# Half of the value pages of a paged attention are multiplied in the gated heads instead of in the attention steps

## The reference

```python
mod = silu(c) @ w_ada + b_ada                       # six shifts, scales and gates
h = rms_norm(x) * (1 + scale1) + shift1
q_a, k_a, v_a, q_g, k_g, v_g, og_g, gk_lr, gate_a, gate_b = split(h @ w_in)
o_a = attend(rms_norm(q_a), rms_norm(k_a), v_a)     # 8 heads of 64
o_g, s_new = gla_chunked(q_g, k_g, v_g, log_a, s0)  # 4 heads, 128 keys, 256 values
o_g = rms_norm(o_g) * silu(og_g)
merged = sigmoid(gate_a) * (o_a @ w_branch_a) + sigmoid(gate_b) * (o_g @ w_branch_b)
x = x + gate1 * (merged @ w_out)
x = x + gate2 * hier_moe(rms_norm(x) * (1 + scale2) + shift2)   # 32 experts, two per token
```

## Time and profile before

| | us |
|---|---|
| median of 3 runs | 1307.64 |
| lowest, highest | 1307.28, 1308.71 |
| profiled execution: span from first to last instruction | 1308.1 |
| TensorE busy in the span | 1183.1 |
| DVE, ScalarE, GpSimd busy | 496.8, 234.5, 234.4 |
| HBM traffic | 354.61 MB read, 22.36 MB written |

### The profile page before, as it was taken

One profiled execution on the slowest core, in us unless ns is written; L12 is line 12 of the kernel. 1 busy time (PEld: TensorE's weight loads), 2 busy tenths in 40 slices (PEclk: granted clock), 3 DMA queues, 4 the chain that ended last, 5 costly groups with the idle time before them and its releaser, 6 DMA issues.

```text
span 1308.1 us, 20837 instructions
## 1 busy us (share of the span) xinstructions
PE 1183.1 (90%) x8041; PEld 746.0 (57%) x8041; DVE 496.8 (38%) x1075; ACT 234.5 (18%) x536; POOL 234.4 (18%) x295
## 2 busy tenths in 40 slices
PE   3999998999999999999999997999987788888797
PEld 2344443475767777688888455666644444444464
DVE  3388966522324243454554456322212111111112
ACT  4122235322323232211001222000000000000000
POOL 2432344201102023340000101111111111111001
PEclk9999999999999999999999997999999999999989
DMA  9998999982654635312624627999999999999994
GB/s 352 372 266 287 364 374 385 377 328 65 251 173 144 171 97 131 97 23 57 177 80 178 257 65 209 403 415 419 411 419 416 418 418 418 417 415 418 415 414 161
DMA packets 118393, 368.17 MB, mean 281 GB/s; under 512 B 12604, under 2 KB 58573, under 8 KB 98966
## 3 DMA queue, kind: packets, MB, share of 16 engines
q1 hardware_dynamic: 93408, 304.44, 60.0%
q0 software_dynamic: 21328, 55.24, 13.7%
q10 hardware_dynamic: 3558, 7.13, 1.8%
HBM read 354.61 MB, written 22.36 MB: 288 GB/s over the span
## 4 chain that ended last, share of the span: by engine, by line
PE 67%; DMA 19%; SPq 6%; DVE 3%; issue 2%; ACT 1%; ACTq 0%; DVEq 0%; POOLq 0%
PE ps L1928 64%; DMA ring<-in_w_exp_gate 9%; SPq L549 4%; DMA hx<-in_w_exp_up 3%; PE ps L1939 3%; DMA hx<-in_w_exp_gate 3%; SPq L554 2%; DMA ring<-in_cache_v 1%; DMA hx<-in_shape_table 1%; DMA h_rows<-ring 1%; DVE work L1548 1%; DVE work L1883 0%; DMA work<-h_rows,idx 0%; DVE work L1658 0%; DVE ring L1655 0%
## 5 line engine op out<-in xcount | busy, mean ns | idle before, releaser
L1928 PE MATMUL ps<-ring,work 128*64 128x256 f32 (+4 forms) x2064 | 296.7, 439 | 42.2 <-DMA ring<-in_w_exp_up 16.5
L1928 PE MATMUL ps<-ring,hx 128*32 128x256 f32 (+3 forms) x1552 | 271.1, 443 | 6.7 <-ACT hx L848 4.2
L1928 PEld LDWEIGHTS ps<-ring,work 128*64 128x64 f32 (+2 forms) x2064 | 157.1, 139 | 163.9 <-issue 84.7
L1928 PEld LDWEIGHTS ps<-ring,hx 128*32 128x32 f32 (+1 forms) x1552 | 157.7, 146 | 102.5 <-issue 78.6
L1928 PE MATMUL ps<-hx,ring 128*128 128x272 f32 x704 | 163.8, 393 | 0.6 <-DVE work L1548 0.6
L1928 PE MATMUL ps<-work 128*32 128x256 f32 (+12 forms) x1186 | 134.9, 399 | 21.6 <-DVE work L1240 9.8
L1928 PEld LDWEIGHTS ps<-hx,ring 128*128 128x128 f32 x704 | 133.0, 190 | 28.7 <-DVE work L1548 1.1
L1928 PE MATMUL ps<-hx,work 128*64 128x256 f32 (+2 forms) x784 | 114.2, 413 | 19.8 <-DMA hx<-in_w_exp_up 10.6
L769 POOL DMA_INDIRECT out<-work x32 | 50.5, 1578 | 327.6 <-DVE work L1893 327.6
L1881 DVE TENSOR_TENSOR work<-work,ps 128x256 f32<-128x256 f32 x32 | 13.5, 421 | 250.2 <-ACT work L1185 250.2
L1928 PEld LDWEIGHTS ps<-hx,work 128*64 128x64 f32 (+2 forms) x784 | 67.9, 144 | 66.1 <-issue 26.4
(11 more groups left out here) (337 smaller groups left out, 948.5 us busy)
## 6 DMA issues: line engine op xcount, KB each, us to landing
ring<-in_w_exp_gate SPq DMA_DIRECT2D x21, 2048.0 KB, 40.8
ring<-in_w_exp_down SPq DMA_DIRECT2D x42, 1024.0 KB, 39.0
ring<-in_w_exp_up SPq DMA_DIRECT2D x21, 2048.0 KB, 40.7
ring<-in_w_ada SPq DMA_DIRECT2D x12, 2048.0 KB, 22.4
hx<-in_w_exp_gate SPq DMA_DIRECT2D x11, 2048.0 KB
hx<-in_w_exp_up SPq DMA_DIRECT2D x10, 2048.0 KB, 40.5
work<-in_w_exp_down SPq DMA_DIRECT2D x20, 1024.0 KB
ring<-in_cache_v SPq DMA_DIRECT2D x64, 256.0 KB, 9.3
```

What stands on the lines that cost most here:

```text
L1928: return pe.matmul(out, lhsT, rhs, start=start, stop=stop, **k)
```

## The change

Value blocks 0 to 7 (the first four sequences) are multiplied in attention steps 1, 2, 4, 5, 7, 8, 10 and 11 (`VALUES_AT`). Blocks 8 to 15 move to the gated stage: four in head 2 and four in head 3, at the place where heads 0 and 1 have `late_ada`, into PSUM bank 5. Since a bank can't be held open through the chunks of a head, their sum is kept in SBUF (`late_values`): ScalarE copies the own tokens' part there in step 17, DVE adds the bank in head 2 and again in head 3, keeps each row's head, and TensorE's `selected` stands in head 3. The weights of the later group are transposed in steps 5, 6, 7 (own tokens) and 17 (pages 8 to 15, into banks 4 and 5); `selected` of the first group moves from step 10 to 13. The stream of loads follows: the late blocks come behind the first weights of heads 2 and 3, `SLOT_ORDER` has other buffers there, and all eight pages of a late block are issued by SyncE. On GpSimd two of the four mixtures of `hT` (`hT_mix`) stand further back in head 3, because their place in SBUF holds `late_values` until then.

```diff
-        SLOT_ORDER = ([3, 1, 2, 0, 4, 5, 3] + [1, 2, 0, EXTRA, 4, 1, 2, 0, 4, 1, 5, 2, 0, 4, 1, 5] + [2, 0, 3, 4, 1] * 3 + [2]
-                      + [0, 3, 4, 1, 2, 5] * 2 + [0, 3, 4, 1] + [2, 5, 3, 4, 0, 2, 3, 5] + [4])
+        SLOT_ORDER = ([3, 1, 2, 0, 4, 5, 3] + [1, 2, 0, EXTRA, 4, 1, 2, 0, 4, 1, 5, 2, 0, 4, 1, 5] + [2, 0, 3, 4, 1, 2, 0, 3]
+                      + [4, 1, 2, 0, 3, 5] * 2 + [4, 2, 0, 3, 5, 1] * 2 + [2, 5, 3, 4, 0, 2, 3, 5] + [4])
...
-        for i in range(DEC_B * PAGES // 8):
-            PAGED[("v", i)] = add_block(("v", i), PAGES // 4, (s("pv_s"), i + 1))
+        EARLY_VALUES = PAGES // 2
+
+        def value_block(i):
+            PAGED[("v", i)] = add_block(("v", i), PAGES // 4 if i < EARLY_VALUES else PAGES // 2, (s("pv_s"), i + 1))
+
+        for i in range(EARLY_VALUES):
+            value_block(i)
         GLA = []
...
+            if h >= 2:
+                for i in range(4):
+                    value_block(4 * h + i)
...
+        SHARED_PAGES = [n for (what, i), n in PAGED.items() if what == "k" or i < EARLY_VALUES]
-            if isinstance(stream[n][1], tuple):
-                paged = [m for m in PAGED.values() if SLOT_ORDER[m] == SLOT_ORDER[n] and m <= n]
+            if n in SHARED_PAGES:
+                paged = [m for m in SHARED_PAGES if SLOT_ORDER[m] == SLOT_ORDER[n] and m <= n]
...
-        cT_kept, prT_high, sc_p = xflat[:, 0:KD * 32], xflat[:, 256:1280], xflat[:, 1280:4352].rearrange("p (z o c) -> p z o c", z=3, o=2)
-        late_mod_rows = [xflat[:, 256:768], xflat[:, 768:1280]]
+        cT_kept, prT_low, sc_p = xflat[:, 0:KD * 32], xflat[:, 256:1280], xflat[:, 1280:4352].rearrange("p (z o c) -> p z o c", z=3, o=2)
+        late_mod_rows = [xflat[:, 1280:1792], xflat[:, 1792:2304]]
+        late_values, prT_high = xflat[:, 2816:3328], xflat[:, 3328:4352]
...
-        TURN_AT, SELECT_AT = 5, 10
+        VALUES_AT = {1: 0, 2: 1, 4: 2, 5: 3, 7: 4, 8: 5, 10: 6, 11: 7}
+        LATER_AT, LAST_LATER_AT, SELECT_AT = {5: 0, 6: 1, 7: 4}, 17, 13
...
-                    sp.wait_ge(s("pv_s"), 2 * PAGES // 2)
+                    sp.wait_ge(s("pv_s"), EARLY_VALUES)
-                    load_pages(sp, n, pieces, range(0, 8, 2), slot_sem)
+                    load_pages(sp, n, pieces, range(0, 8, 2) if n in SHARED_PAGES else range(8), slot_sem)
...
+                    pool.wait_ge(s("pv_s"), EARLY_VALUES + 4)
...
+                    if h == GH - 1 and n == 0:
+                        pool.wait_ge(s("o_sel"), 2)
+                        pool.tensor_tensor(hT_mix[:, 2], hT[:, low, first], hT[:, low, last], ALU.subtract).then_inc(s("hT_mixed"), 1)
+                    if h == GH - 1 and n == 1:
+                        pool.wait_ge(s("hT_mixed"), 2)
+                        pool.tensor_tensor(hT_mix[:, 3], hT[:, high, first], hT_mix[:, 1], ALU.subtract).then_inc(s("hT_mixed"), 1)
...
+                if z in LATER_AT:
+                    later_weights(LATER_AT[z])
+                if z == LAST_LATER_AT:
+                    later_weights(2)
+                    later_weights(3)
+                    act.wait_ge(*after("own_late_ps"))
+                    act.activation(late_values, ps[:, 0, :], ACT.Copy).then_inc(*done("own_late"))
...
-            sample_heads(1)
...
+                if h == GH - 1:
+                    sample_heads(1)
...
+                elif h == 2:
+                    dve.wait_ge(*after("own_late"))
+                    dve.wait_ge(s("pv_s"), EARLY_VALUES + 4)
+                    dve.tensor_tensor(late_values, late_values, ps[:, VALUE_BANK, :], ALU.add).then_inc(*done("values_low"))
+                else:
+                    dve.wait_ge(*after("values_low"))
+                    dve.wait_ge(s("pv_s"), EARLY_VALUES + 8)
+                    link(dve.tensor_tensor(late_values, late_values, ps[:, VALUE_BANK, :], ALU.add))
+                    heads_kept(late_values, late_values)
...
+            def own_values(stop):
+                for j in range(4):
+                    last = mm(ps[32 * j:32 * j + 32, 0, :], pr_own[0:NS, 32 * j:32 * j + 32], v_tok[0:NS, PT, :], True, stop,
+                              skip_group_check=True)
+                return last
+
...
+            def late_page_values(first):
+                pe.wait_ge(s("pr_T"), 10)
+                for v in range(first, first + 4):
+                    page_values(v, VALUE_BANK, v == first, v == first + 3)
...
+                if z in LATER_AT:
+                    pe.wait_ge(s("l_norm"), 2)
+                    pe.wait_ge(s("p_ov"), z - 3)
+                    later_weights_turned(LATER_AT[z], 1)
+                if z == LAST_LATER_AT:
+                    pe.wait_ge(s("sc_max"), UNITS - 1)
+                    later_weights_turned(2, 4)
+                    later_weights_turned(3, 5)
...
+                if z == LAST_LATER_AT - 1:
+                    pe.wait_ge(s("o_rows"), 1)
+                    pe.wait_ge(s("pr_T"), 8)
+                    own_values(True).then_inc(*done("own_late_ps"))
+                if z in VALUES_AT:
+                    v = VALUES_AT[z]
+                    if v == 0:
+                        pe.wait_ge(s("pr_T"), 5)
+                        own_values(False)
+                    page_values(v, 0, False, v == EARLY_VALUES - 1)
...
+            pe.wait_ge(s("pr_T"), 10)
...
-            selected(1)
-            pe.wait_ge(s("oa_taken"), 2)
+            pe.wait_ge(*after("own_late"))
...
+                    late_page_values(EARLY_VALUES)
+                else:
+                    late_page_values(EARLY_VALUES + 4)
...
+                        if h == GH - 1:
+                            pe.wait_ge(s("o_rows"), 2)
+                            selected(LATE_BANK, late_values)
...
+                    if i == 0:
+                        pe.wait_ge(*(after("mod_middle") if h == 0 else (s("mod_set"), 2) if h == 1 else after("late_rows") if h == 2 else (s("oa_taken"), 2)))
+                    if i == 0 and h == 2:
+                        pe.wait_ge(*after("values_low"))```

The order of TensorE's instructions, from the scores of step 14 (`ps<-work 128x384`) to the transposes of step 17. `32x512` from `ring` are value blocks, `cst,hx` transposes of the weights, `ring,work 64x128` products with the values. Before:

```order
106 L1928 MATMUL ps<-work 128x384 x2
107 L1928 MATMUL ps<-ring,hx 32x512 x8
108 L1939 MATMUL ps<-cst,hx 128x128 x2
109 L1928 MATMUL ps<-ring,work 64x128 x8
110 L1928 MATMUL ps<-work 128x512 x2
111 L1928 MATMUL ps<-ring,hx 32x512 x8
112 L1939 MATMUL ps<-cst,hx 128x128 x4
113 L1928 MATMUL ps<-ring,work 64x128 x2
114 L1928 MATMUL ps<-ring,hx 32x512 x8
115 L1939 MATMUL ps<-cst,hx 128x128 x6
116 L1928 MATMUL ps<-ring,work 64x128 x4
117 L1939 MATMUL ps<-cst,hx 128x128 x8
```

More of the change, by code:

```diff
@@ L307, in layer_kernel @@
         rbw, far_hot = rbw[0:BUCKETS + 1, 0:P], rbw[0:BUCKETS + 1, P:2 * P]
-        qT, kT, v_tok, near, logit0, logit1, prT_low, pr_own = carve(
+        qT, kT, v_tok, near, logit0, logit1, _, pr_own = carve(
             2176, PAIRS * NT, PAIRS * NT, 5 * AW, AH * 2 * P, PAST + NS, PAST + NS, 2 * 512, P)
@@ L685, in _ @@
                     pool.dma_start(near[COPIES * a:COPIES * a + COPIES], src).then_inc(s("near_in"), 16)
-            for i in range(KEY_BLOCKS):
+            for i in range(EARLY_VALUES):
                 half_pages("v", i)
+            first, last = token_half
+            low, high = GATE_A.low, GATE_A.high
             for h in range(GH):
@@ L696, in _ @@
                     pool.wait_ge(s("late_out"), 64)
-                    first, last = token_half
-                    low, high = GATE_A.low, GATE_A.high
+                    pool.wait_ge(s("pv_s"), EARLY_VALUES + 4)
                     pool.tensor_tensor(hT_mix[:, 0], hT[:, low, last], hT[:, high, last], ALU.add).then_inc(s("hT_mixed"), 1)
@@ L2164, in page_values, with selected @@
                         q = 4 * (page % 2) + j
-                        last = mm(ps[32 * j:32 * j + 32, 0, :], page_weights(g, page)[:, 32 * j:32 * j + 32], slot(n)[:, AW * q:AW * q + AW],
-                                  False, page == PAGES - 1, skip_group_check=True)
+                        last = mm(ps[32 * j:32 * j + 32, bank, :], page_weights(g, page)[:, 32 * j:32 * j + 32], slot(n)[:, AW * q:AW * q + AW],
+                                  start and page == 2 * i, stop and page == 2 * i + 1, skip_group_check=True)
                 last.then_inc(s("pv_s"), 1)
-            def selected(g):
-                pe.wait_ge(s("o_rows"), g + 1)
-                if g:
-                    pe.wait_ge(s("oa_taken"), g)
-                    pe.wait_ge(s("p_T"), UNITS)
-                else:
-                    pe.wait_ge(s("p_ov"), SELECT_AT - 3)
+            def late_page_values(first):
+                pe.wait_ge(s("pr_T"), 10)
+                for v in range(first, first + 4):
+                    page_values(v, VALUE_BANK, v == first, v == first + 3)
+            def selected(bank, rows):
```

(2 more changed lines are left out.)

71 lines of the change are left out of this document (29 added, 42 removed).

## The result

| | before | after |
|---|---|---|
| median of 5 runs each | 1308.71 | 1316.60 |
| lowest, highest | 1307.28, 1313.19 | 1316.00, 1319.60 |
| profiled execution, span | 1308.1 | 1314.8 |
| TensorE, DVE, GpSimd busy in the span | 1183.1, 496.8, 234.4 | 1186.3, 497.6, 217.1 |
| mean granted clock of the profiled execution | 0.982 | 0.978 |

The change makes the kernel slower: ratio 1.0061, 95% interval 1.0046 to 1.0076, which is 6.0 to 9.9 us. The sign is the predicted one, the size is not: 1316.6 lies 5.0 above the forecast of 1311.6 and 1.6 above the top of the range. Of the 5.0, 1.1 is the base: the forecast added its 4 to a median of three runs, 1307.64, and the five runs here have 1308.71. The other 3.9 is the change itself, 7.9 instead of 4.

What follows compares the result with a forecast made beforehand. TensorE was taken as the bound, 67% of the chain of waits. Attention -10.6 and gated heads +15.1 gave +4.5, less 0.5: +4 on a median of 1307.64, so 1311.6 us, range 1307.0 to 1315.0.

Steps and rivals of the forecast that it cites:

- Steps 1 to 11, -6.9: Early attention steps: three blocks' 5.6 us go, 2.2 come back as waits, and some work moves to later steps; net -6.9.
- Steps 12 to 18, -2.6: Last attention steps: blocks -9.3, old waits -1.7, moved groups +3.2, new waits +5.2; net -2.6 us.
- the 0.5 taken off: Taken from the +4.5 sum because the step 12 to 18 walk counts short waits at full length; leaves +4.
- The four waits: New TensorE waits in steps 12 to 18, mostly behind ScalarE's copies: 1.5, 1.3, 1.9 and 0.45, together 5.2 us.
- Behind the steps, -1.1: Between attention steps and gated stage: a 1.06 us selection goes, the wait for ScalarE's copy becomes 0.9 from 1.01.
- The clock. I take this as unchanged: Attention steps: the clock fall at 206 to 209 us, costing 1.7 us, was expected to stay as it was.
- Rival (c): The clock falls in attention steps 12 to 16, costing 1.7 us, so 1313.3; chance 0.16.
- The second fall that was foreseen, in step 3: Step 3's missing block makes a gap of about 2 us; a clock fall there would cost next to nothing.
- The heads, +15.1: Last two gated heads: value blocks 13.9, selection 1.0, wait behind it 0.2; range 14.9 to 15.3 us.
- Loads: Late value pages and first merging weights arrive in time, the weights with 20 us of room; no cost.
- Outside these the stages keep their lengths: Sign: beyond attention steps, the last two heads and the later merging start, no stage changes its length.
- The signs it gave: Gated stage starts near 257, merging near 549; TensorE idle before the gates grows 6 to 7 us, wrong if under 3.

Runs made afterwards that it cites:

- step 3 filled: The changed kernel with filler matmuls in attention steps 15 and 16 and eight more in step 3; 1316.73 us, ratio 1.0042 to the kernel before.
- the attention steps alone: The changed kernel with most of the late value blocks' products left out of the last two gated heads; 1303.63 us, ratio 0.9959 to the kernel before.
- the six later ones: Six runs of the changed kernel without further edit, beside the kernel before on the same chip; 1315.41 us, ratio 1.0061.
- the two single ones: Two more profiled executions of the unedited changed kernel, one timed run each; 1313.50 and 1315.92 us.
- the delay of 4.3: The kernel before with 20 filler matmuls of 512 columns in the last gated head; 1314.73 us, ratio 1.0045.

## Why the prediction went wrong, step by step

**Steps 1 to 11, -6.9: right.** The scores that open the last pair of heads start 52.61 behind the start of attention (231.90 in the rows above), 59.55 before (239.69 in the earlier trace rows): -6.94. Step 3's block was indeed lost again: the wait for DVE ends 25.26 behind the start (204.55), 25.27 before (205.41).

**Steps 12 to 18, -2.6: right in its terms, wrong with the clock.** From there to the last products (253.17, and 262.72 before) it is 21.27 against 23.03, only -1.8. Less the 1.50 that the fall cost it is 19.77, or -3.3, against a forecast of -2.6 and the 0.5 taken off at the end. The same holds in each execution of the change: 22.14, 21.20 and 24.14 less 2.37, 1.44 and 4.37 (two falls, 2.84 and 1.53) give 19.77, 19.76 and 19.77. So all that differs between these tails is the clock. The four waits sum to 4.9, forecast 5.2. **Behind the steps, -1.1: right** (3.99 against 5.07).

**"The clock. I take this as unchanged": this step failed.** The forecast put the clock in the last steps at nothing. It weighed only the fall at 205 and let the evidence of waits of 0.3 to 0.9 us stand for waits of 1.2 to 1.8. The last two of these have 2 us of work between them (243.22 to 245.24), and behind them the clock is 0.50 for 3 to 7 us in every execution, at a price of 1.4 to 2.8 us. The trace of the kernel before had this pattern already. Among the waits of the attention steps the forecast left one out:

```profile
200.64 0.85 PE L1939 MATMUL ps<-cst,hx 128*128 128x128 f32 x6 [1.19 <-DVE hx L1435]
```

It stands 2.1 us of work ahead of the wait of 2.71, and behind the two comes the fall of the earlier trace rows. Rival (c) is the mechanism that came, and I gave it 0.16; its price of 1.7 was near, its time of 1313.3 is still 3.3 short. Against it I had put that TensorE stays over half busy; that did not keep the clock. The Trainium skill, "TensorE: Matmul & The Clock Gate", section "HAM oscillation", tells of a kernel whose bursts of about 2 us lie between waits of 3 to 5 us and start slow each time; I drew on it and went against it. The traces agree in the effect and go further, since the waits here are shorter than in its case: TensorE was busy 3.78 of the 5 us from 240 and 3.22 of the next 5.

The second fall that was foreseen, in step 3, came in the first profile (195 to 199) and in two of the other three. DVE's work covered it: with step 3 filled the next wait for DVE ends 25.25 behind the start, and 25.26 with the fall. Where it lasted longest, to 201, the wait at the later place was down to 0.94 and the fall at 205 did not come.

**The 0.5 taken off: right in size.** Without the fall the attention steps of the first profile give 11.3 (87.65 less 76.37), the walk's 10.6 and the half microsecond. One trace of the kernel before differs from the next by up to 1.3, so the half as such isn't shown.

**The heads, +15.1: right**, 14.8 against each trace where the clock didn't fall at their start (0.1 under the range given), 13.74 of it in the blocks and 0.8 in the selection; what is left, 0.2, is what the forecast had for the wait behind it, so GpSimd's moved subtractions cost nothing, as forecast. **Loads: right**, with room to spare. SyncE had issued the 32 pages of head 3 by 474.7 and they are used at 507.88; DVE takes up the first merging weights without a wait:

```profile
439.17 35.53 SPq L534 DMA_DIRECT2D ring<-in_cache_v  x32
```

```profile
542.60 0.68 DVE L1476 TENSOR_TENSOR ring<-ring 128x512 f32<-128x512 f32 x1
```

**"Outside these the stages keep their lengths": not always.** In the first profile, and with step 3 filled, a load of two transfers of 128 KB, issued by ScalarE at 729.60, 1 to 3 us after SyncE had issued 6 MB of activations and experts' weights, landed late; DVE waited for it, TensorE for DVE, and the clock fell:

```profile
740.99 0.68 DVE L1691 TENSOR_TENSOR ring<-ps,work 32x512 f32<-32x512 f32 x1 [4.72 <-DMA work<-late_mod_rows]
```

```profile
745.18 0.59 PE L1975 MATMUL ps<-cst,ring 32*128 32x32 f32 x4 [1.60 <-DVE ring L1696]
```

It cost 2.8 there and 4.5 in the other, against the 24.3 of the change's other traces. A shorter one is in the trace of the attention steps alone, where DVE waited 3.87 for the same load and 0.3 was lost. That makes three of the eight traces of kernels with the new order of loads (one of four of the change itself) and none of six with the old. With so few, whether the change makes it likelier stays open.

**The signs it gave.** The gates' first product was to come near 257 (257.16) and the main part of the merging stage near 549 (548.78). The second agrees by luck: the fall had cost 1.5, and the attention steps had started 0.85 early (179.29 against 180.14). The other sign was an idle time 6 to 7 us longer, wrong if under 3. The windows of the whole attention stretch, of the kernel after and of the kernel before:

```profile
179.29:257.16 77.87, 65.55 (x590) 34.95 (x587) 53.58 (x121) 38.67 (x99) 10.30 (x19) 0.93 0.82 289
```

```profile
180.14:267.79 87.65, 78.95 (x727) 37.11 (x723) 54.86 (x122) 38.60 (x99) 26.35 (x49) 0.98 1.05 381
```

Idle time is 12.3 against 8.7, only 3.6 more. Busy time fell by 13.4, where blocks and selection of 14.9 + 1.06 went: 2.6 us more for the same work, at a clock of 0.93 against 0.98. The two together are 6.2. Where the clock moves, idle time alone was a poor sign.

**The sum.** By the traces the change costs 5.8: the forecast's 4; 2.0 for the clock in the attention steps; -0.8 in the heads, of which 0.5 is the fall in one trace of the kernel before; and 0.6 that the other stages are longer in the mean. The first five timed runs have 7.9, the six later ones 6.6 in the medians and 8.0 by the ratio [5.5, 10.3], the two single ones about 6. So about 1 to 2 us of the first result are not placed by any trace. An execution like the first profile, with its late transfer, would have 2.8 of it; the delay of 4.3 shows an excess of the same size in its timed runs (5.9) and none in its trace. Its cause stays open.

The base has a part in the miss as well. The prediction set the span of the profile, 1308.1, beside times of runs and found it near their median. In all runs that list both, the time is 1.7 to 1.9 above the span, so the profiled execution was one of about 1309.9 (an estimate), above all three of those runs. Later medians of the kernel before are 1308.7 to 1309.8, 1.1 to 2.2 above the base that the forecast took.

## What to carry to other kernels

Work that fills an engine's wait is free where it is and costs its full price where the engine has no wait: before moving matmuls to a stretch with free DMA, ask whether that stretch has a free TensorE. When TensorE's steps lose their filling, price the waits that come back and then the clock behind them, at once, above all where two waits of over a microsecond stand close together with little work between. And a kernel whose waits for pages are small may still be just ahead of its loads: here the gain was given back until half of the loads had been moved.

## What the runs showed of the hardware

- Waits of 1.2 and 1.8 us with 2 us of work between them lowered the granted clock from 1.00 to 0.50 (2.4 to 1.2 GHz) in five of five traces that had both; with both filled it stayed at 1.00, in two traces. With waits of 0.16 and 2.50 at these places it fell too, so it isn't shown that it takes two.
- A wait's length alone doesn't tell. The single wait of 1.45 us (233.84) left the clock at 1.00 in seven of the eight traces that have it and lowered it in one (233 to 236). In the kernel before, waits of 1.23 and 1.39 for a page left it at 1.00, and the wait of 1.01 ahead of the gates lowered it in one of six traces.
- Waits of 1.77 and 1.87 us behind full stretches brought it down: 1.92 became 3.27 and 3.50 us for a value block.
- A fall cost 1.4 to 2.8 us where no other engine covered it. Less its price, the last steps take 19.77 us in each of the four executions, within 0.01.
- Adding 14 matmuls, 3.7 us of TensorE's time, made the attention steps 1.7 us shorter than the mean without them.
